# Turned norms worked on by quarters instead of by row blocks

## What is computed

```python
# first block
h = rms_norm(x, norm_mix);          z = h @ w_in                       # then three kinds of attention and gating
x = x + concat(out_a, out_b, out_c) @ w_out
h = rms_norm(x, norm_xattn);        m = rms_norm(mem, norm_mem)
q = h @ xattn_wq;                   kv = m @ xattn_wkv
x = x + attention(q, kv) @ xattn_wo
h = rms_norm(x, norm_mlp)
x = x + square(relu(h @ w_up)) @ w_down
x = rms_norm(x, final_norm)
# second block, ctx is a second input of 256 tokens
h_lat = rms_norm(x, norm_mix_g) * (1 + scale) + shift
h_ctx = rms_norm(ctx, norm_mix_g) * (1 + scale) + shift
...                                                                    # gated scan and windowed attention
x = x + gate * (concat(...) @ w_out_2)
h = rms_norm(x, norm_ffn_g) * (1 + scale) + shift
x = x + gate * ((silu(h @ w_gate) * (h @ w_up)) @ w_down_2)
```

## Time and profile before

| what | value |
|---|---|
| time, median of 3 runs | 2848.02 us (2843.61 to 2851.54) |
| the profiled execution's own time | 2849.79 us |
| its span | 2848.0 us |
| TensorE busy | 2733.1 us, 96% |
| VectorE busy | 1844.2 us, 65% |
| ScalarE busy | 1259.1 us, 44% |
| mean granted TensorE clock | 0.98 of full |
| weights and inputs read | 568 MB, 200 GB/s over the span |

### The profile page before, as it was taken

The page is one execution under the profiler, slowest core; times in us unless marked ns, Lnnn a source line. Parts: engine busy times, 40 slices in busy tenths (PEclk is TensorE's granted clock), DMA queues, the critical chain, the costliest instruction groups (busy, mean ns, idle before and its releaser), DMA issues.

```text
span 2848.0 us, 34264 instructions
## 1 busy us (share of the span) xinstructions
PE 2733.1 (96%) x13606; PEld 2294.0 (81%) x13606; DVE 1844.2 (65%) x2461; ACT 1259.1 (44%) x1646; POOL 56.8 (2%) x77
## 2 busy tenths in 40 slices
PE   7999999989999999999799999999989999999999
PEld 6899888878888888778588788777768888888887
DVE  5657756566787787776766775656566666554555
ACT  3333555445434434344555455434344444434433
POOL 0000000000000000000000000101000000000000
PEclk9999999999999999999999999999989999999999
DMA  6776655557778777766576755434247777666665
GB/s 213 239 231 219 193 177 156 156 179 250 241 256 250 242 248 247 276 223 202 173 225 213 223 178 143 132 108 128 89 129 241 246 249 246 185 189 192 186 194 174
DMA packets 303008, 572.51 MB, mean 201 GB/s; under 512 B 20381, under 2 KB 30001, under 8 KB 302465
## 3 DMA queue, kind: packets, MB, share of 16 engines
q1 hardware_dynamic: 299712, 559.77, 62.9%
q0 software_dynamic: 2960, 10.48, 1.3%
q10 hardware_dynamic: 176, 0.07, 0.0%
HBM read 568.16 MB, written 2.10 MB: 200 GB/s over the span
## 4 chain that ended last, share of the span: by engine, by line
PE 80%; DVE 7%; ACT 5%; DMA 4%; issue 4%; SPq 0%; ACTq 0%; DVEq 0%
PE ps L1614 22%; PE ps L1616 22%; PE ps L1615 21%; ACT whi L1881 3%; DMA raw<-in_w_in 2%; PE ps L1608 2%; PE ps L1609 2%; PE ps L1610 2%; DVE wlo L2163 2%; DMA raw<-in_w_down 1%; PE ps L1569 1%; DVE acc L2181 1%; PE ps L1797 1%; PE ps L1817 1%; DVE yb L2211 1%
## 5 line engine op out<-in xcount | busy, mean ns | idle before, releaser
L2163 DVE TENSOR_TENSOR wlo<-raw,whi 128x1024 fp32r<-128x1024 f32 x857 | 1044.4, 1225 | 692.7 <-ACT whi L1881 683.3
L1881 ACT ACTIVATE whi<-raw 128x1024 fp32r<-128x1024 f32 x857 | 900.2, 1056 | 1042.5 <-PE ps L1616 285.5
L1614 PE MATMUL ps<-whi,th 128*128 128x512 f32 (+2 forms) x3168 | 1265.1, 399 | 59.5 <-DVE wlo L2163 34.1
L1616 PE MATMUL ps<-whi,tl 128*128 128x512 f32 (+2 forms) x3168 | 1238.3, 391 | 0.0
L1615 PE MATMUL ps<-wlo,th 128*128 128x512 f32 (+2 forms) x3168 | 1236.4, 390 | 0.0
L1614 PEld LDWEIGHTS ps<-whi,th 128*128 128x128 f32 x3168 | 605.3, 191 | 189.2 <-DVE wlo L2163 43.7
L1616 PEld LDWEIGHTS ps<-whi,tl 128*128 128x128 f32 x3168 | 604.2, 191 | 125.9
L1615 PEld LDWEIGHTS ps<-wlo,th 128*128 128x128 f32 x3168 | 606.0, 191 | 117.8 <-issue 1.9
L2181 DVE SCALAR_TENSOR_TENSOR acc<-raw,silc,acc 128x512 f32<-128x512 f32 x480 | 344.4, 749 | 65.8 <-DMA raw<-in_w_mod 60.4
L1608 PE MATMUL ps<-th,whi 128*128 128x256 f32 x640 | 188.6, 295 | 6.2 <-DVE wlo L2163 6.2
L1609 PE MATMUL ps<-th,wlo 128*128 128x256 f32 x640 | 183.7, 287 | 0.0
(11 more groups left out here) (276 smaller groups left out, 1413.5 us busy)
## 6 DMA issues: line engine op xcount, KB each, us to landing
raw<-in_w_in SPq DMA_DIRECT2D x240, 512.0 KB, 4.0
raw<-in_w_down SPq DMA_DIRECT2D x216, 512.0 KB, 4.7
raw<-in_w_mod SPq DMA_DIRECT2D x192, 512.0 KB, 3.8
raw<-in_w_gate_up SPq DMA_DIRECT2D x176, 512.0 KB, 3.7
raw<-in_w_up SPq DMA_DIRECT2D x128, 512.0 KB, 4.0
raw<-in_w_out SPq DMA_DIRECT2D x64, 512.0 KB, 3.9
raw<-in_xattn_wkv SPq DMA_DIRECT2D x16, 512.0 KB, 3.7
raw<-in_xattn_wq SPq DMA_DIRECT2D x8, 512.0 KB, 3.6
```

Of the source, the lines that this page charges most:

```text
L1614: pe.matmul(p, xh, wh[:, c, c0:n], start=a and (form == "rows" or tb == 0), stop=False, skip_group_check=True)
L1616: ins = pe.matmul(p, xl, wh[:, c, c0:n], start=False, stop=z, skip_group_check=True)
L1881: self.e.activation(t.his[g % NHI][:, 0:n], t.raws[j % NRAW][:, 0:n], ACT.Copy).then_inc(*s.hi.up(g))
L2163: self.e.tensor_tensor(t.los[j % NRAW][:, 0:n], t.raws[j % NRAW][:, 0:n], t.his[g % NHI][:, 0:n].bitcast(F), ALU.subtract).then_inc(*s.lo. ...
```

## The change

`turn_piece` loses its last stage, which becomes a function `turn_low` of its own. In `turn`, the low halves of both row blocks are now written when the second row block of a quarter has passed stages 1 to 4. In turns with `whole=True` (the default: `mem`, `xa`, `mlp`, `ctx`, `lat`) a step goes straight on from the first row block to the second, so one step makes a quarter, and the empty steps behind it become `1 + 2 * rest`, so that the mean pace stays; they are left out in a hurry. `x` and `ffn` are called with `whole=False` and keep a step for each piece. Nothing is computed differently.

```diff
-    def turn(self, name, src, landed, rs, op, g, sh, gtok, rest=0, ease=False, lag=1):
+    def turn(self, name, src, landed, rs, op, g, sh, gtok, rest=0, ease=False, lag=1, whole=True):
...
+            def low(j):
+                self.turn_low(name, j, op)
+                self.yb_after[j % 2] = [(s.tl, (name, j))]
+                for kt in range(4 * (j // 2), 4 * (j // 2) + 4):
+                    op.ready[kt] = op.ready[kt] + [(s.tl, (name, j))]
+                op.pieces = j + 1
+
             for j, (q, tb) in enumerate(pieces):
                 if rs is not None:
                     scale(j + 2)
...
                 bank.give((s.tg, (name, j)))
-                self.yb_after[j % 2] = [(s.tl, (name, j))]
-                for kt in range(4 * q, 4 * q + 4):
-                    op.ready[kt] = op.ready[kt] + [(s.tl, (name, j))]
-                op.pieces = j + 1
+                if tb:
+                    low(j - 1)
+                    low(j)
+                elif whole:
+                    continue
                 yield
-                for _ in range(rest):
+                for _ in range(1 + 2 * rest if whole else rest):
+                    if op.hurry:
+                        break
                     yield
...
-        self.turn("x", self.x_part, lambda q, tb: self.xb[2 * q + tb], None, op1, t.gain["mix"], None, [(s.cols, "mix")], lag=0)
+        self.turn("x", self.x_part, lambda q, tb: self.xb[2 * q + tb], None, op1, t.gain["mix"], None, [(s.cols, "mix")], lag=0, whole=False)
...
-        self.turn("ffn", self.x_part, lambda q, tb: at[2 * q + tb], rs, opf, t.gmod[:, 0, :], t.mod[:, 48:64], [(s.gs, "ffn")] + self.mod_cols(12, 16))
+        self.turn("ffn", self.x_part, lambda q, tb: at[2 * q + tb], rs, opf, t.gmod[:, 0, :], t.mod[:, 48:64], [(s.gs, "ffn")] + self.mod_cols(12, 16), whole=False)
...
+
+    def turn_low(self, name, j, op):
+        s, q, tb = self.s, j // 2, j % 2
+        y = self.t.yb[tb][:, :].rearrange("p (a b) -> p a b", a=4)
         self.wait_ge(*s.th.at((name, j)))
         at = slice(4 * q, 4 * q + 4), slice(128 * tb, 128 * tb + 128)
-        dv.tensor_tensor(op.l[:, at[0], at[1]], y, op.h[:, at[0], at[1]].bitcast(F), ALU.subtract).then_inc(*s.tl.up((name, j)))
+        self.e.tensor_tensor(op.l[:, at[0], at[1]], y, op.h[:, at[0], at[1]].bitcast(F), ALU.subtract).then_inc(*s.tl.up((name, j)))
```

More of the change, by code:

```diff
@@ L343 @@
     start_loads = load_mem_part = load_consts = columns_rest = spread_rstd = mem_square = heads_direct = finish = load_x_part = late_loads = load_ctx = load_final = load_masks = load_bounds = load_qkg = skip
-    issue = columns = split = mod_add = mod_total = multiply = turn_scale = turn_piece = stat = root = reduce_sums = skip
+    issue = columns = split = mod_add = mod_total = multiply = turn_scale = turn_piece = turn_low = stat = root = reduce_sums = skip
     heads_silu = rows_out = residual_add = spatial_weights = skip
```

## The result

| | median of before | median of this | ratio, with its 95% interval |
|---|---|---|---|
| the changed kernel | 2846.21 us (2843.61 to 2851.54, 4 runs) | 2814.30 us (2810.16 to 2817.40, 4 runs) | 0.9881 [0.9865, 0.9897] |
| the same, run again | 2845.30 us | 2813.24 us | 0.9886 [0.9871, 0.9901] |
| the same, a third time | 2846.40 us | 2816.18 us | 0.9898 [0.9881, 0.9914] |

The change makes the kernel about 32 us faster (31.9 between the medians of the first row). The forecast was 2824 us with a range from 2817 to 2839. Over its twelve runs the changed kernel has a median of 2814.3 us.

What follows compares the result with a forecast made beforehand. TensorE bounds the kernel, by its own work plus the time it stands still, and the change touches only the second. Gains of 12.7 + 6.9 + 4.9 + 1.4 = 25.9 us from 2849.8 give 2824 us, range 2817 to 2839.

Steps and rivals of the forecast that it cites:

- the two new waits of `mlp`: TensorE waits 1.6 us at the fourth product of `w_up` and 1.3 us more after the third quarter.
- `mlp`: Part 1: three `tl` waits with their clock, 15.6 us, go, less 2.9 of new waits: 12.7 us gained, bounds 9 to 15.6.
- `lat`: Part 2: VectorE and ScalarE need 6.7 us a quarter in place of 8.4: 6.9 us gained, bounds 2 to 9.
- `mem` and `xa`: Part 3: VectorE loses fourteen gaps, more than TensorE's waits there: 4.9 us gained, bounds 0 to 4.9.
- `ffn`: Part 4: the first product's second low half comes sooner, later steps keep their pace: 1.4 us gained, bounds −1 and 2.
- `x`: Part 5, at the start: nothing gained; no waits, and the third y starts at 10.5 as before.
- `ctx`: Part 5: nothing gained; VectorE's burst of 4.0 us is covered by three split pieces of 2.84 us.
- The two waits for `xn`: In two quarters of `lat`, the second transposes wait 1.2 to 1.3 us for a scaling, inside the 6.7 us pace.
- Rival 1: Whole kernel: nothing won, TensorE is the bound and each wait returns under another name; 2850 us, chance 0.13.
- Rival 2: Half won: new waits at `mlp` and `lat` pass 2 us and bring the low clock; 2838 us, chance 0.20.
- Rival 3: Slower: in `ctx` and `lat`, second transposes wait for `xn` behind the first `th`; 2858.4 us, chance 0.04.
- Rival 4: More won: the two new waits of `mlp` don't appear; 2819 us, in the forecast's own range, no separate chance.

Runs made afterwards that it cites:

- Experiment 3: The kernel before with the change in `mem` and `xa` alone: 2839.14 us, ratio 0.9972.
- experiment 1: The changed kernel with whole quarters in one step but each low half straight behind its own y (unpaired): 2834.47 us against 2845.53 of before, ratio 0.9956.
- experiment 5: The kernel before with the change in `x`, `ctx` and `ffn` alone: 2841.37 us against 2847.40, ratio 0.9980.
- experiments 8 and 9: The changed kernel with `ffn` turned by quarters, one quarter ahead of the first product: 2814.91 us; then two quarters ahead: 2812.47 us, run again 2808.08 us.
- experiment 7: The changed kernel with both scalings of the next quarter issued ahead of the first `th` in `ctx` and `lat`: 2816.74 us, ratio 0.9882 to before.
- experiment 4: The kernel before with the change in `lat` alone: 2839.91 us, ratio 0.9979.

## Why the mechanism was right, and where the forecast was too small

**The order of size was right in each large part**, and the two new waits of `mlp` were found in advance by walking the new order with the old durations. By term, forecast and measured: `mlp` 12.7 and 12.9; `lat` 6.9 and 7.1; `mem` and `xa` 4.9 and 7.0; `ffn` 1.4 and 1.4, with up to 2.5 us of clock on top; `x` 0 and 1.0 to 1.3; `ctx` 0 and nothing that can be told from what varies. The measured ones sum to 29.4 to 29.7 us, and to 31.9 to 32.2 with `ffn`'s clock, against 31.9 between the medians; 25.9 were forecast.

**Where the forecast started.** Of the 9.6 us between 2823.9 and 2814.30, 6.0 are gain that the sum hadn't, and 3.6 are its starting point: it took off from the profiled execution of 2849.8 us, where the median of the four runs of before is 2846.21.

**`mem` and `xa`: the step that failed.** "I take **4.9**, bounds 0 to 4.9" took the idle time of the rows as the ceiling. Experiment 3 shows that it isn't: each of the six waits costs 0.2 to 0.3 us more than its row, and the bursts spare another 0.6 us. The same omission is in the other parts, for one wait in `mlp`, but nowhere so large, since here the idle time comes in many short waits. That the whole idle time would go was right, as was its reason, that VectorE's fourteen gaps are larger than it: with the gaps kept, in experiment 1, most of the waits stay.

**`x`: the step that failed.** It was put at nothing, and `x` was listed as having no wait. That overlooked the 4.94 us that TensorE waits for the first `wlo` on L1608 (experiment 5), which is not on the line of the earlier trace rows. "In `x` the third y starts at 10.5 as before, since the second piece landed late" was wrong too. VectorE's timeline of the changed kernel:

```profile
8.32 1.47 DVE L2232 TENSOR_TENSOR tl<-yb,th 128x512 fp32r<-128x512 f32 x2
9.77 0.69 DVE L2221 TENSOR_TENSOR yb<-ps,cols 128x512 f32<-128x512 f32 x1
12.10 2.36 DVE L2173 TENSOR_TENSOR wlo<-raw,whi 128x1024 fp32r<-128x1024 f32 x2 [1.64 <-ACT whi L1891]
```

It starts at 9.77, and the low half that stood behind it is gone from the way of the first `wlo`, at 12.10. The arrival of the piece was not the last cause before; the gaps ahead of the two low halves before it were.

**`ffn`: the wait was right, and the clock came on top.** The first product waited 2.61 us for the 4.00 of before: 1.39 us less, as forecast, and it starts 1.38 to 1.41 us earlier in all nine profiles with the pairs in `ffn`. The other 2.5 of the 3.9 us are clock, in two places. The first product, to the start of the next, took 5.0 us for 5.9; but in `lat` alone and in quarters unpaired, which leave `ffn` as it was, it took 4.8 and 4.7 us, so those 0.9 us need no change in `ffn`. The other 1.6 us are behind the last wait, of 2.2 us in all kernels but those of experiments 8 and 9. In before the granted clock there is 0.57, in the changed kernel 1.00. The windows 2120.85 to 2123.69 of before and 2088.80 to 2091.61 of after (us, busy us by engine, granted clock, DMA):

```profile
2120.85:2123.69 2.84, 2.84 (x8) 2.22 (x9) 2.36 (x2) 1.02 (x2) 0.00 (x0) 0.57 0.32 123
```

```profile
2088.80:2091.61 2.81, 2.81 (x12) 2.33 (x13) 2.36 (x2) 1.03 (x2) 0.00 (x0) 1.00 0.25 96
```

In eleven profiles with this wait the clock was low behind it in five and full in six, with and without the change in `ffn`. So what is shown as `ffn`'s own is 1.4 us; that the clock behind its last wait stayed full in all three profiles of the changed kernel is luck as far as these runs can tell, and whether its shorter first wait helps the first product's clock stays open.

**`lat`: the right size by a working that was partly wrong.** I had 6.7 us for a quarter, so products 3.3 us apart. Two of the quarters took 8.1 (experiment 7's rows): 6.7 and 1.4 of two modulation sums, which I had left out. They are in the kernel before as well (at 1377.42 and 1391.47), so they drop out of the difference. The gain came, 3.9 us of it up to the product at 1405.65 of before and 3.2 behind it, where TensorE had waited 1.44 and 2.68 us for `wlo` and VectorE now arrives earlier. The two waits for `xn` came, 1.54 us each where 1.2 to 1.3 was forecast, and cost nothing (experiment 7).

**Rival 1** (nothing is won) is out: the time fell by 32 us, with TensorE the busiest engine before and after. The page's rule that went with it, the Trainium skill's "Perfetto Trace Analysis", § Identifying the Most-Contended Engine, would have left the time where it was, as the prediction read it. What the same page of the Trainium skill says next, in § Optimization Strategy, this case bears out: look at the gaps on that engine within a regime, and at what would end them sooner. Of the 20.5 us of standing still that went, 17.4 were waits for `wlo` and `tl`.

**Rival 2** (half is won, since the new waits bring the low clock) rests on a price that was not paid. The low clock did come: behind the 1.96 us wait it was 1.00 in the first profile and 0.64 in the second of the same kernel, where product and transposes took 4.72 us (us, busy us, granted clock, DMA):

```profile
567.58:572.30 4.72, 4.72 (x15) 0.64 0.50 191
```

Yet `mlp` is −13.3 in both, as in all nine profiles with the change in it, of which four had a clock of 0.63 to 0.66 there. In the second profile the next wait, 1.35 us for `tl`, isn't there. The lost time fell into a wait that VectorE ended anyway, as in experiment 4. So the 1.8 us of clock for this new wait were not to be paid, and behind the second one of `mlp` and the two of `lat` the clock was 1.00. The same reading doesn't take the 1.6 us out of the gain, in "10.3 + 5.3 = 15.6": before, the slow product and the 4.38 us behind it went together, and where the clock stayed full (experiment 4) the waits were longer by as much. What was wrong in the working is "2.03 us is the shortest that I found with a lower one": in the kernel before the clock also fell behind a wait of 1.52 us, at 1520.43 us (4.21 us from the first to the twelfth matmul's start, granted clock 0.63), and behind one of 1.98 us for `xn`, at 1396.61.

**Rival 3** (slower, since the second four transposes wait for `xn`) is out: in `ctx` there is no such wait, and in `lat` the two cost nothing. **Rival 4**'s condition didn't come: both new waits did.

**The range** began at 2817 because its sum of best cases, 31.5 us, had 4.9 as the most for `mem` and `xa` and nothing for `x`, and was taken from 2848.0. With 7.0 and 1.3 it would have begun at 2813, and at 2811 from the median of 2846.2. Two other figures of the prediction don't add up: rival 4 is 25.9 + 2.9 = 28.8 us, so 2821 and not 2819, and the worst bounds of the parts, 9 + 2 + 0 − 1 = 10 us, give 2840 and not 2832.

## What to carry to other kernels

Where a helper engine's chain (make, round, subtract) is on the path, issue the independent halves of two pieces together and run the whole loop once for both: the pairs alone and the bigger step alone gave 0.0 and 1.6 us in `lat`, both gave 7.1. If TensorE and the helper then wait for each other in turn, give the helper a lead of one unit (3.9 us became 10.1 in `ffn`). When a wait of TensorE is to be removed, count its idle time and 0.2 to 0.3 us more. Count clock lost behind it only if no wait for the same helper follows, or if that wait goes too; a clock lost in front of a wait that stays is taken up by it.

## What the runs showed of the hardware

- A wait of TensorE behind a product costs 0.16 us ahead of it and 0.08 to 0.18 us in the next product more than the idle time in the rows (166 waits at full clock). Behind transposes it costs 0.24 us, all ahead of it, since the product there is 0.12 us longer without a wait as well.
- Whether the clock falls behind a wait of about 2 us is not settled by its length. In the fourteen profiles 33 products of twelve matmuls stand behind a wait of 1.9 to 2.3 us. From the start of the first matmul to that of the twelfth it was 2.6 to 2.7 us in 19 of them, 4.2 in 12 and 3.7 in two. The place counts: behind the 2.61 us wait of `ffn`'s first product, which comes after one of 5.3 us and twelve transposes, the clock was low in all six profiles that have it (3.5 to 4.4 us), and behind 2.64 to 2.68 us in `lat` it was full in four of five. The Trainium skill, "TensorE: Matmul & The Clock Gate", Part 1, says that the number of slow matmuls at the start of a kernel differs from run to run. Here the same is seen behind a wait in the middle of one: the profiles of the changed kernel have 1.00 and 0.64 behind the same 1.96 us. The modulation total near 1242 us of before shows it once more: a wait of 2.77 us and a clock of 1.00 behind it, and in the changed kernel 2.67 us and 0.50. Those 1.6 us are most of the +2.7 us in its column.

```profile
1242.00:1243.78 1.78, 1.78 (x17) 1.78 (x17) 1.78 (x2) 1.78 (x2) 0.00 (x0) 1.00 1.00 346
```

```profile
1218.21:1221.62 3.41, 3.41 (x17) 3.41 (x17) 3.33 (x4) 3.38 (x4) 0.00 (x0) 0.50 0.97 359
```

- What makes it fall in one run and not in the next stays open.
